# Last stage of a decoder-layer kernel merged into the expert block, with the sum of the two expert rows on GpSimd

## The reference

```python
y = routed_experts(h, idx, gw, w_gate, w_up, w_down)   # per token: the rows of its two experts, weighted, added
x = x + g2[:, None, :] * y                             # x is the residual stream after the mixer ("x1")
return rms_norm(x, final_norm_w)                       # x * rsqrt(mean(x*x) + 1e-6) * final_norm_w
```

## Time and profile before

| | us |
|---|---|
| median of 3 runs | 3262.5 |
| profiled execution: its own time | 3264.45 |
| profiled execution: span from first to last instruction | 3262.8 |
| issue of the last scatter (L1760) | 3166.64 |
| first load of the last stage issued (L1993) | 3176.40 |
| first DVE instruction of the last stage (L2023) | 3183.82 |
| last store issued (L2012) | 3258.49 |

### The profile page before, as it was taken

One profiled execution on the slowest core, in us unless ns is written; L12 is line 12 of the kernel. 1 busy time (PEld: TensorE's weight loads), 2 busy tenths in 40 slices (PEclk: granted clock), 3 DMA queues, 4 the chain that ended last, 5 costly groups with the idle time before them and its releaser, 6 DMA issues. The chain is left out here.

```text
span 3262.8 us, 36512 instructions
## 1 busy us (share of the span) xinstructions
PE 2833.7 (87%) x12749; PEld 2292.8 (70%) x12749; DVE 2464.7 (76%) x1827; ACT 1499.0 (46%) x1234; POOL 573.5 (18%) x444
## 2 busy tenths in 40 slices
PE   2699999999996767899964899999999999999970
PEld 2577777777874655677854788878887788778850
DVE  5977888876545993678645788888888888888859
ACT  4122222212112331000031788888888888878852
POOL 0210000000003553455500111111111111111100
PEclk7799999999998888999965899999999999999985
DMA  8712112225521115777762798999888999899968
GB/s 311 260 39 69 53 57 71 58 60 171 163 69 52 48 33 192 234 222 245 230 246 116 287 363 361 376 383 377 355 354 353 394 395 364 355 375 381 379 247 369
DMA packets 248421, 771.98 MB, mean 237 GB/s; under 512 B 25176, under 2 KB 119432, under 8 KB 179516
## 3 DMA queue, kind: packets, MB, share of 16 engines
q1 hardware_dynamic: 185618, 613.76, 49.7%
q10 hardware_dynamic: 50810, 115.73, 10.3%
q0 software_dynamic: 11952, 41.97, 3.2%
HBM read 733.62 MB, written 82.84 MB: 250 GB/s over the span
## 5 line engine op out<-in xcount | busy, mean ns | idle before, releaser
L1915 DVE TENSOR_TENSOR wlo<-wraw,whi 128x2048 fp32r<-128x2048 f32 x444 | 1006.4, 2288 | 181.6 <-ACT whi L1864 181.5
L1864 ACT ACTIVATE whi<-wraw 128x2048 fp32r<-128x2048 f32 x444 | 843.4, 1916 | 245.0 <-PE ps L1849 115.3
L1795 PE MATMUL ps<-whi,xhi 128*128 128x512 f32 x1184 | 475.2, 401 | 0.0
L1797 PE MATMUL ps<-whi,xlo 128*128 128x512 f32 x1184 | 462.9, 391 | 0.0
L1796 PE MATMUL ps<-wlo,xhi 128*128 128x512 f32 x1184 | 462.2, 390 | 0.0
L358 PE MATMUL ps<-hh,wih 128*128 128x512 f32 x1152 | 372.2, 404 | 27.6 <-POOL hl L310 18.7
L358 PE MATMUL ps<-hl,wih 128*128 128x512 f32 x1152 | 363.9, 397 | 0.0
L358 PE MATMUL ps<-hh,wil 128*128 128x512 f32 x1152 | 362.9, 396 | 0.0
L657 DVE SCALAR_TENSOR_TENSOR acc<-u,vcur,acc 128x1024 f32<-128x1024 f32 x240 | 308.3, 1285 | 7.7
L358 PEld LDWEIGHTS ps<-hh,wih 128*128 128x128 f32 x1152 | 217.8, 190 | 90.2 <-POOL hl L310 19.5
L333 ACT ACTIVATE wih<-wraw_i 128x1024 fp32r<-128x1024 f32 x72 | 76.1, 1057 | 401.6 <-PE ps L358 317.0
(11 more groups left out here) (327 smaller groups left out, 4394.5 us busy)
## 6 DMA issues: line engine op xcount, KB each, us to landing
wraw<-in_w_gate_dram SPq DMA_DIRECT2D x148, 1024.0 KB, 6.8
wraw<-in_w_up_dram SPq DMA_DIRECT2D x148, 1024.0 KB, 7.6
wraw<-in_w_down_dram SPq DMA_DIRECT2D x148, 1024.0 KB, 7.6
slot<-in_w_mod_dram ACTq DMA_DIRECT2D x96, 512.0 KB, 4.8
wraw_i<-in_w_in_dram SPq DMA_DIRECT2D x72, 512.0 KB, 3.9
wmA<-in_w_mod_dram SPq DMA_DIRECT2D x48, 512.0 KB, 5.6
wraw_o<-in_w_out_dram SPq DMA_DIRECT2D x64, 256.0 KB, 4.4
y<-ybuf_d SPq DMA_DIRECT2D x16, 1024.0 KB, 12.1
```

The source lines that it names most:

```text
L1795: pe.matmul(dst, xhi[:, t, :], whi[:, s, w], start=(t == 0), stop=False)
L1797: last = pe.matmul(dst, xlo[:, t, :], whi[:, s, w], start=False, stop=(t == KT - 1))
L1864: act.activation(whi[:, spl(m), :], wraw[:, raw(m), :], ACT.Copy).then_inc(s_whi, 1)
L1915: dve.tensor_tensor(wlo[:, spl(m), :], wraw[:, raw(m), :], whi[:, spl(m), :].bitcast(F32), ALU.subtract).then_inc(s_wsp[raw(m)], 1)
```

## The change

The last stage no longer has a Block, a barrier and tiles of its own. Its instructions are appended to each engine's list in the expert block.

- **x1.** All eight tiles of x1 are loaded inside the expert block: tiles 0 and 1 into `xf` as before, tiles 2 to 7 into the six weight slots `wraw`, each as soon as DVE has split the last piece that lay there (pieces 1, 6, 8, 9, 10, 11 of the last item).
- **Buffers.** `y1`, `y2` and `of` lie over the memory of `whi` and `wlo`, `junk3` over `xhi`.
- **The start.** SP waits for the last scatter's semaphore `s_os` itself and then issues the y loads, without a barrier between.
- **The sum of the two expert rows** goes from DVE to POOL, as eight 128x2048 additions; DVE waits for each (`s_ya`). The other two steps of `combine`, `finish`, and ACT's part are unchanged.

```diff
-        s_fr, s_xf = sem("final_w_loaded"), [sem(f"x1_reloaded{b}") for b in range(2)]
+        s_fr, s_xf = sem("final_w_loaded"), [sem(f"x1_reloaded{j}") for j in range(TT)]
+            w_at = (nc.sbuf_base + 31) // 32 * 32
             whi = sb(st, "whi", [P, NSPL, D], F32R)
             wlo = sb(st, "wlo", [P, NSPL, D], F32R)
...
+            y1 = nc.alloc_sbuf_tensor_at("y1", [P, 3, D], F32, offset=w_at)
+            y2 = nc.alloc_sbuf_tensor_at("y2", [P, 3, D], F32, offset=w_at + 12 * D)
+            of = nc.alloc_sbuf_tensor_at("of", [P, 2, D], F32, offset=w_at + 24 * D)
+            junk3 = nc.alloc_sbuf_tensor_at("junk3", [P, D], F32, offset=junk_at)
...
+            FREED = (1, 6, 8, 9, 10, 11)
+
+            def x1_tile(j):
+                return xf[:, j, :] if j < 2 else wraw[:, (FREED[j - 2] + 1) % NRAW, :]
...
                     sp.dma_start(frow[:], bcast(final_norm_w, D)).then_inc(s_fr, 16)
-                    for b in range(2):
-                        sp.dma_start(xf[:, b, :], x1_d[b * P:(b + 1) * P, :]).then_inc(s_xf[b], 16)
+                    for j in range(TT):
+                        if j >= 2:
+                            m = FREED[j - 2]
+                            sp.wait_ge(s_wsp[raw(m)], raw_turn(n, m) + 1)
+                        sp.dma_start(x1_tile(j), x1_d[j * P:(j + 1) * P, :]).then_inc(s_xf[j], 16)
+                    sp.wait_ge(s_os, 16 * n + 16)
+                    for j in range(TT):
+                        b = j % 3
+                        if j >= 3:
+                            sp.wait_ge(s_sum3, j - 2)
+                        sp.dma_start(y1[:, b, :], ybuf_d[j * P:(j + 1) * P, :]).then_inc(s_y1[b], 16)
+                        sp.dma_start(y2[:, b, :], ybuf_d[SEQ + j * P:SEQ + (j + 1) * P, :]).then_inc(s_y1[b], 16)
...
                     pool.wait_ge(s_os, 16 * n + 16)
+                    for j in range(TT):
+                        pool.wait_ge(s_y1[j % 3], 32 * (j // 3) + 32)
+                        pool.tensor_tensor(y1[:, j % 3, :], y1[:, j % 3, :], y2[:, j % 3, :], ALU.add).then_inc(s_ya, 1)
...
-        ph56.close()
-        ph24.close()
-        with ExitStack() as st:
-            with nc.Block() as block:
...
                     def combine(j):
-                        b = j % 3
-                        dve.wait_ge(s_y1[b], 32 * (j // 3) + 32)
-                        order(dve.tensor_tensor(y1[:, b, :], y1[:, b, :], y2[:, b, :], ALU.add))
-                        order(dve.tensor_tensor(y1[:, b, :], y1[:, b, :], g2row[:], ALU.mult))
-                        if j < 2:
-                            dve.wait_ge(s_xf[j], 16)
-                        else:
-                            dve.wait_ge(s_xs[j - 2], 16)
-                        dve.tensor_tensor(x1_tile(j), x1_tile(j), y1[:, b, :], ALU.add).then_inc(s_sum3, 1)
+                        dve.wait_ge(s_ya, j + 1)
+                        order(dve.tensor_tensor(y1[:, j % 3, :], y1[:, j % 3, :], g2row[:], ALU.mult))
+                        dve.wait_ge(s_xf[j], 16)
+                        dve.tensor_tensor(x1_tile(j), x1_tile(j), y1[:, j % 3, :], ALU.add).then_inc(s_sum3, 1)
```

More of the change, by code:

```diff
@@ L1675, in hybrid_layer @@
             xrow = sb(st, "xrow", [P, D])
+            junk_at = (nc.sbuf_base + 31) // 32 * 32
             xhi = sb(st, "xhi", [P, KT, P], F32R)
@@ L1694, in hybrid_layer @@
                 sem("hidden_split"), sem("out_rows_ready"), sem("out_rows_stored"))
+            y1 = nc.alloc_sbuf_tensor_at("y1", [P, 3, D], F32, offset=w_at)
+            y2 = nc.alloc_sbuf_tensor_at("y2", [P, 3, D], F32, offset=w_at + 12 * D)
+            of = nc.alloc_sbuf_tensor_at("of", [P, 2, D], F32, offset=w_at + 24 * D)
+            junk3 = nc.alloc_sbuf_tensor_at("junk3", [P, D], F32, offset=junk_at)
+            ssq3 = sb(st, "ssq3", [P, TT])
+            rst3 = sb(st, "rst3", [P, TT])
+            s_y1 = [sem(f"y_loaded{b}") for b in range(3)]
+            s_ya, s_sum3, s_sq3, s_std3, s_of3, o_p7 = (
+                sem("y_added"), sem("residual_combined"), sem("combined_squared"), sem("combined_std"),
+                sem("final_ready"), sem("p7_order"))
+            s_out = [sem(f"out_stored{b}") for b in range(2)]
+            FREED = (1, 6, 8, 9, 10, 11)
+            def x1_tile(j):
+                return xf[:, j, :] if j < 2 else wraw[:, (FREED[j - 2] + 1) % NRAW, :]
             BANK_G, BANK_U, BANK_D, BANK_H, BANK_X = 0, 512, 1024, 3072, 3584
@@ L1911, in _ @@
                     work(n, last=True)
+                    for j in range(TT):
+                        act.wait_ge(s_sum3, j + 1)
+                        if j >= 1:
+                            act.wait_ge(s_sq3, j)
+                        act.activation(junk3[:], x1_tile(j), ACT.Square, accum_out=ssq3[:, j:j + 1]).then_inc(s_sq3, 1)
+                        act.wait_ge(s_sq3, j + 1)
+                        act.activation(rst3[:, j:j + 1], ssq3[:, j:j + 1], ACT.Sqrt, bias=epsc[:], scale=1.0 / D).then_inc(s_std3, 1)
+                        if j >= 1:
+                            act.wait_ge(s_of3, j)
+                            act.dma_start(out[(j - 1) * P:j * P, :], of[:, (j - 1) % 2, :]).then_inc(s_out[(j - 1) % 2], 16)
+                    act.wait_ge(s_of3, TT)
+                    act.dma_start(out[(TT - 1) * P:TT * P, :], of[:, (TT - 1) % 2, :]).then_inc(s_out[(TT - 1) % 2], 16)
+                    for b in range(2):
+                        act.wait_ge(s_out[b], 16 * (TT // 2))
                 def split_w(dve, i, m, last=False):
@@ L1962, in _ @@
                     work(n, last=True)
-        ph56.close()
-        ph24.close()
-        with ExitStack() as st:
[L1969 to L1984, removed]
-            with nc.Block() as block:
-                @block.sync
-                def _(sp):
-                    for j in range(TT):
-                        b = j % 3
[L1991 to L2017, removed]
@@ L2045, in _ @@
                     finish(TT - 1)
+        ph56.close()
+        ph24.close()
 _INS = ["x", "c", "w_mod", "b_mod", "norm1_w", "w_in", "conv_dw_w", "conv_dw_b", "conv_ln_w", "conv_ln_b",
```

## The result

The changed kernel is slower: a median of 3267.4 us over 20 runs against 3259.1 us over 20 runs of the kernel before, ratio 1.0026 with a 95% interval of 1.0017 to 1.0034. The forecast was 3271.7 us with a range of 3260 to 3277, that is +9.2 us or a ratio of 1.0028; the medians differ by 8.3 us. Single executions of one kernel spread over 14 us (before) and 19 us (changed), so a difference of this size can be told only from many of them.

A forecast was written before the change was run, and what follows sets the result against it. Bound: DVE's four wide instructions per tile in the last stage, plus the handover before it. Handover -6.5, first addition +4.5, seven more +29.8, DVE's eight steps -18.6: +9.2 us on median 3262.5, so 3271.7 us, range 3260 to 3277.

The forecast's parts named there:

- handover: Between last scatter and last stage: y loads go out at about 3169.9 instead of 3176.4, 6.5 us earlier.
- landing of y0: Start of the last stage: from first y load's issue to y0's arrival stays 7.4 us.
- first addition on the path: Last stage's start: DVE must wait for POOL's first 128x2048 addition, +4.5 us.
- seven blocked DVE instructions: Last stage: each of POOL's seven later additions holds up DVE by 4.25 us, +29.8 us together.
- eight DVE additions gone: Last stage: DVE loses eight y1 + y2 steps of 2.32 us, -18.6 us.
- price of a turn: Last stage: DVE's loss per POOL addition when both read SBUF and alternate, 4.25 us, read from other stages' overlaps.
- even tile of about 11.2 us: Last stage, sign in the changed profile: with DVE and POOL taking turns, a tile takes about 11.2 us.
- 7 us for each reload of y: Last stage: reloading a y pair takes 5.0 us for 2 MB plus about 2 of start, so turns are never empty.
- Rival 1: Last stage: POOL and DVE run side by side, a tile takes 7.0 us, -20.6 us, 3241.9 us; chance 0.14.
- Rival 2: Last stage: turns, but each POOL addition takes only 3.6 us; +2.0 us, 3264.5, no change; chance 0.13.
- Rival 3: Handover: x1 loads hold up scatter or y loads until about 3176, no gain there; +15.7, 3278.2 us; chance 0.07.
- drain: POOL's drain of 6.19 us, moved to the kernel's end, fits beside DVE's last tile and store; 0 taken, bound +6.2.

The follow-up runs named there:

- e1: The changed kernel with the addition of the two expert rows given back to DVE; ratio 0.9974 to the kernel before, stretch 89.5 us.
- e2: The kernel before, its Block, barrier and x1 loads kept, with only the addition moved to POOL; ratio 1.0049 to the kernel before, stretch 111.5 us.
- e3: The changed kernel with each POOL addition replaced by three memsets of y2, which write SBUF and read none; one execution, stretch 78.9 us.
- e4: The changed kernel with g2row and frow copied to PSUM by ACT and read there by DVE; ratio 0.9984 to the kernel before, stretch 89.4 us.
- e8: e4 with four y buffers instead of three, POOL's additions not held back; one execution, stretch 88.9 us.
- e6: e8 with POOL's addition for tile j held back until x1 + y1 of tile j-2 is done; ratio 0.9957 to the kernel before, stretch 80.1 us.
- e5: e1 with x1 tiles 2 to 7 loaded in the last stage again; ratio 0.9974 to the kernel before, stretch 89.6 us.

## Why the prediction was right

| step of the prediction | predicted, us | measured, us | by |
|---|---|---|---|
| handover | -6.5 | -6.6 | first y load 3.2 behind the scatter; e1 |
| landing of y0 | 7.4, unchanged | 7.5 | POOL's start |
| first addition on the path | +4.5 | +4.6 | 3179.14 to 3183.74 |
| seven blocked DVE instructions | +29.8 | +29.3 | records of 6.41 to 6.60; e2, e3 |
| eight DVE additions gone | -18.6 | -18.6 | unblocked steps unchanged |
| sum | +9.2 | +8.7 | stretch; medians +8.3 |

The mechanism and each of its terms held. The absolute time is 4.3 us under the forecast of 3271.7, and 3.4 of these are not the change's: the forecast stood on the kernel before at 3262.5, the median of three executions, and over twenty it is 3259.1. The forecast had put the line between slower and no change at 3269, and 3267.4 lies under it; that the change is slower is shown by the ratio against the twenty.

- **The price of a turn.** 4.25 us each was forecast, 4.18 measured. It was read from overlaps of other shapes; the rule carried over to tensor_tensor of 128x2048 without a correction. I had named about eight blocked instructions where there are seven; the sum had seven. Seven collisions were not certain: in e4 and e8, where POOL also starts as soon as a pair has landed, the loss per collision is 0.5 to 4.2 us, because only one of three instructions can be blocked there. The even tile of about 11.2 us was not what came (7.0 to 15.4), nor the 7 us for each reload of y (7.2 to 11.8); neither is a term of the sum.
- **Rival 1, side by side,** would have been true for a POOL that only writes (e3) or for DVE forms with a PSUM operand (e4, e6). It is false for this kernel because all three of DVE's instructions read two tiles from SBUF.
- **Rival 2, a cheap addition:** it takes 4.48 us alone, so no.
- **Rival 3, the x1 loads in the way:** they fill the DMA engines to just past 3168, about when the scatter is issued (3168.48), and the first y load still goes out 3.2 us behind it; nothing is pushed back. The margin was as thin as forecast. e1 and e5, with and without the six early loads, have the same stretch.
- **The drain,** which I took as hidden, is: it ends 12 us before DVE. It reads 12.46 us there, 6.2 beside the last addition and 6.3 behind it. The forecast had tied the 6.19 us to a scatter directly ahead; they come all the same when additions stand between, and are hidden only because DVE goes on for longer.

The largest miss of this study is not in the prediction but in e4's expectation, and its cause is shown by e6 and e8: where the additions fall in DVE's tile.

## What to carry to other kernels

Before moving an elementwise operation from VectorE to GpSimd, look at what the remaining VectorE instructions read: if both operands lie in SBUF and GpSimd's operation reads SBUF too, the two engines take turns, and an operation of 2.3 us on VectorE comes back as 4.2 us. Give VectorE a PSUM operand, and place GpSimd's work beside instructions that have one, by a wait if need be; that turned a loss of 0.26% into a gain of 0.53%. About half of this gain is the handover, which e1 has without any work on POOL (0.26%); the placed additions bring the stretch from e1's 89.5 to 78.1 us. And a block's end behind a scatter from GpSimd can cost more than the scatter (6.2 us of drain, 3.2 us to land): waiting for the transfer's own semaphore was worth 6.6 us by itself.

## What the runs showed that was not expected

- A blocked instruction counts as busy. DVE's busy share in the last stage is as high after the change as before (59.65 of 60 us from 3190 to 3250, before 59.34); only the records' lengths tell. A maximum far above the median in a line's durations is the sign.
- A producer that runs as soon as it can may hit the worst place. In e4 and e8 POOL starts as soon as data lands, and it lengthened the one instruction that it could block in seven and in five of eight tiles.
- Stages before the change ended up to 11 us apart between profiled executions of kernels that are alike up to there (last scatter at 3157.47 in e4, 3168.48 in the changed kernel). It is why the stretch behind the scatter was compared. The twenty executions of the changed kernel point at TensorE's clock: the mean granted clock is 0.933 in the shortest (3258.6 us) and 0.925 to 0.928 in the three longest (3275.0 to 3277.2), with the others between. No run varied the clock by itself, so the cause is not shown.
